# Two pairs of column blocks of the convolution's input computed with seven block products for eight at 9 of 32 channel pairs

## The reference

```python
h = rms_norm(x, norm_g[l])
proj = jnp.einsum('bsd,dn->bsn', h, w_in[l])
(aq, ak, av, ai, af, ao, az,
 bcq, bk, bv, bki, bwi, bz,
 cqkv, cb, ca, cz) = jnp.split(proj, split_points, axis=-1)
...
qkv = jax.nn.silu(causal_depthwise_conv(cqkv, d_conv_w[l]))
```

## Time and profile before

| | |
|---|---|
| median of 3 runs | 1528.72 us |
| the profiled execution's own time | 1529.63 us |
| its span | 1527.8 us |
| TensorE busy | 1523.5 us, 100%, 6960 matmuls |
| VectorE busy | 1044.1 us, 68% |
| ScalarE busy | 781.0 us, 51% |
| GpSimd busy | 362.9 us, 24% |
| read from HBM | 312.81 MB |
| granted TensorE clock, mean | 1.000 |

### The profile page before, as it was taken

One profiled execution on the slowest core, in us unless ns is written; L12 is line 12 of the kernel. 1 busy time (PEld: TensorE's weight loads), 2 busy tenths in 40 slices (PEclk: granted clock), 3 DMA queues, 4 the chain that ended last, 5 costly groups with the idle time before them and its releaser, 6 DMA issues.

```text
span 1527.8 us, 18922 instructions
## 1 busy us (share of the span) xinstructions
PE 1523.5 (100%) x6960; PEld 1261.3 (83%) x6960; DVE 1044.1 (68%) x1608; ACT 781.0 (51%) x1039; POOL 362.9 (24%) x608
## 2 busy tenths in 40 slices
PE   9999999999999999999999999999999999999999
PEld 7888888888888887888878888888888888888887
DVE  6647555666759865576569677676555877788883
ACT  6745444487544444554545545544445555454543
POOL 9041112230230030126420254344300011110000
PEclk9999999999999999999999999999999999999999
DMA  9886778886788875458765787798876677667667
GB/s 288 286 239 195 224 215 230 217 232 182 227 249 251 252 221 169 147 184 282 246 201 172 228 250 204 236 274 255 231 245 189 191 220 212 190 223 222 210 203 193
DMA packets 207980, 339.35 MB, mean 222 GB/s; under 512 B 53097, under 2 KB 60568, under 8 KB 207632
## 3 DMA queue, kind: packets, MB, share of 16 engines
q1 hardware_dynamic: 184784, 288.66, 62.1%
q0 software_dynamic: 23056, 49.47, 12.4%
q10 hardware_dynamic: 48, 0.02, 0.0%
HBM read 312.81 MB, written 28.73 MB: 224 GB/s over the span
## 4 chain that ended last, share of the span: by engine, by line
PE 98%; DVE 1%; ACT 0%; issue 0%; DMA 0%; DVEq 0%
PE acc L1186 29%; PE acc L1189 29%; PE acc L1188 28%; PE mix L1189 1%; PE mix L1188 1%; PE mix L1186 1%; PE mix L1293 1%; PE mix L1376 1%; PE acc L1202 1%; PE acc L1204 1%; PE acc L1203 1%; PE mix L1204 1%; PE mix L1203 1%; PE mix L1202 1%; PE mix L1365 0%; PE mix L1286 0%
## 5 line engine op out<-in xcount | busy, mean ns | idle before, releaser
L1879 DVE TENSOR_TENSOR w_lo<-w_raw,w_hi 128x1024 fp32r<-128x1024 f32 (+2 forms) x523 | 629.2, 1217 | 356.5 <-ACT w_hi L1517 352.9
L1517 ACT ACTIVATE w_hi<-w_raw 128x1024 fp32r<-128x1024 f32 (+2 forms) x523 | 542.9, 1049 | 436.9 <-PE acc L1189 346.1
L1186 PE MATMUL acc<-w_hi,op_hi 128*128 128x512 f32 (+1 forms) x1868 | 734.2, 393 | 0.3 <-DVE w_lo L1879 0.3
L1189 PE MATMUL acc<-w_hi,op_lo 128*128 128x512 f32 (+1 forms) x1868 | 726.9, 389 | 0.0
L1188 PE MATMUL acc<-w_lo,op_hi 128*128 128x512 f32 (+1 forms) x1868 | 726.7, 389 | 0.0
L1186 PEld LDWEIGHTS acc<-w_hi,op_hi 128*128 128x128 f32 x1868 | 350.8, 188 | 73.9 <-issue 1.3
L1189 PEld LDWEIGHTS acc<-w_hi,op_lo 128*128 128x128 f32 x1868 | 350.6, 188 | 73.5
L1188 PEld LDWEIGHTS acc<-w_lo,op_hi 128*128 128x128 f32 x1868 | 350.9, 188 | 70.8
L888 POOL DMA_DIRECT2D conv_dram<-y x48 | 30.6, 690 | 169.3 <-ACT y L1580 168.5
L888 POOL DMA_DIRECT2D y_dram<-y x32 | 20.6, 716 | 120.2 <-DVE y L2198 68.6
L1049 POOL DMA_DIRECT2D bp_dram<-b_ps x48 | 31.4, 712 | 67.4 <-ACT b_ps L1749 64.0
(11 more groups left out here) (455 smaller groups left out, 1312.4 us busy)
## 6 DMA issues: line engine op xcount, KB each, us to landing
w_raw<-in_w_in_dram SPq DMA_DIRECT2D x367, 512.0 KB, 4.6
w_raw<-in_w_out_dram SPq DMA_DIRECT2D x128, 512.0 KB, 4.5
w_raw<-in_w_in_dram SPq DMA_DIRECT2D x16, 384.0 KB, 3.3
w_raw<-in_a_wuq_dram SPq DMA_DIRECT2D x12, 512.0 KB, 5.7
out_dram<-in_x_dram POOLq DMA_DIRECT2D x7, 512.0 KB, 6.3
conv_dram<-y POOLq DMA_DIRECT2D x48, 64.0 KB, 3.9
y<-conv_dram POOLq DMA_DIRECT2D x48, 64.0 KB, 4.7
w_raw<-in_a_wuqi_dram SPq DMA_DIRECT2D x6, 512.0 KB, 4.7
```

The lines of the kernel that those rows point to most:

```text
L1186: nc.tensor.matmul(o, hi[:, kt, tok], hv[:, i, n0:n1], start=(kt == (kts if late else blk["kts"])[0]), stop=False)
L1189: last_mm = nc.tensor.matmul(o, lo[:, kt, tok], hv[:, i, n0:n1], start=False, stop=(kt == blk["kts"][-1]))
L1517: func(split_ap(w_hi, c), w_raw[:, c % RAW_BUFS, 0:n], ACT.Copy).then_inc(hi_ready, 1)
L1879: vec.tensor_tensor(split_ap(w_lo, c), w_raw[:, c % RAW_BUFS, 0:n], split_ap(w_hi, c).bitcast(F32), ALU.subtract).then_inc(lo_ready, 1)
```

## The change

conv 2 and 3, and conv 4 and 5, become two pairs as well. The first uses seven products at channel pairs 0 to 4, the second at 0 to 3, nine in all. `CONV_ORDER` gives the order of the chunks: 1 is a chunk of the pair's first column block alone, 2 one of the second, S a channel pair in both columns, with seven products. The first pair is chunks 32 to 63; its S pairs are chunks 36/37, 42/43, 48/49, 52/53, 56/57. The second is chunks 64 to 95, with S at 66/67, 72/73, 78/79, 84/85. The number of chunks and their bytes stay the same. For the sums of x VectorE first adds `op_hi` and `op_lo` again (`xs`), makes the four sums, ScalarE makes their high part (`xh`) and VectorE the low part (`xl`), for five channel pairs, in steps 17 to 27. The ScalarE pieces `evac` of conv 2 to 5 go; in their place come `evs` and `evx` (ScalarE scales the combined products, two operations of 128x1024) once per pair and `evn` on VectorE (two operations of 128x512) per column block. The gate for `cd` and `conv` moves with the end of the blocks.

```diff
-SEVEN = [[8, 9, 10, 11, 12], [8, 9, 10, 11, 12, 13, 14]]
+SEVEN = [[0, 1, 2, 3, 4], [0, 1, 2, 3], [8, 9, 10, 11, 12], [8, 9, 10, 11, 12, 13, 14]]
+CONV_SINGLE = 2
+CONV_ORDER = ["1211S1111S1112S22S22S122222", "12S1111S1111S1122S1222222222"]
+X_S = SEVEN[0]
...
-    for j in range(6):
+    for j in range(CONV_SINGLE):
         project("conv", j, C_CQKV + 512 * j)
+    for j in range(CONV_SINGLE, 6):
+        p, q = (j - CONV_SINGLE) // 2, (j - CONV_SINGLE) % 2
+        plain, seven = [i for i in range(KT // 2) if i not in SEVEN[p]], iter(SEVEN[p])
+        of_column = iter(plain)
+        kts = [2 * i + a for token in CONV_ORDER[p] if token in ("S", "12"[q])
+               for i in [next(seven) if token == "S" else next(of_column)] for a in range(2)]
+        block("cpair", j, "h", kts, wide, 512, "w_in", C_CQKV + 512 * j)
...
+        if x["kind"] == "cpair":
+            p, q = (x["arg"] - CONV_SINGLE) // 2, x["arg"] % 2
+            if q:
+                of_seven = [c for c, (b_, kts) in enumerate(chunks) if b_ == b and kts[0] // 2 in SEVEN[p]]
+                woven[of_seven[0] - 2].append(("four", p))
+                woven[of_seven[-1]] += [("evs", p), ("evx", p)]
+            woven[last[b]].append(("evn", (p, q)))
...
+    for n, i in enumerate(X_S):
+        for name, more in (("xs", 0), ("xh", 1), ("xl", 2)):
+            woven[NX + 1 + 2 * n + more].append((name, i))
+    at = 0
     for j in range(6):
-        at = weave((end("conv", j) if j else FIRST_EVAC) + (12 if j < 5 else 9), [("cd", 2 * j), ("cd", 2 * j + 1)])
-        at = weave(at, [("conv", 2 * j), ("conv", 2 * j + 1)], 3 if j < 5 else 2)
+        ended = (FIRST_EVAC, end("conv", 1))[j] if j < CONV_SINGLE else end("cpair", j)
+        at = weave(max(at, ended + (12 if j < 5 else 9)), [("cd", 2 * j), ("cd", 2 * j + 1)])
+        at = weave(at, [("conv", 2 * j), ("conv", 2 * j + 1)], 3 if j < 4 else 2)
...
+            def evx(p, use):
+                act.wait_ge(rstd_ready, 1)
+                if p == 0:
+                    for use in four_mix(p):
+                        act.wait_ge(emptied[use % 4], use // 4 + 1)
+                else:
+                    for q in range(2):
+                        wait_acc_read(act, p, q)
+                for m in range(M):
+                    func(pair_sum(p)[:, m], pair_sum(p)[:, m], ACT.Copy, scale=rstd[:, m:m + 1]).then_inc(pair_scaled, 1)
...
+            def xs_sums(i, use):
+                raw = x_raw(i)
+                hi, lo = [v[:, 2 * i:2 * i + 2, :].rearrange("p k t -> p (k t)") for v in (op_hi, op_lo)]
+                step(vec.tensor_tensor(raw, hi.bitcast(F32), lo.bitcast(F32), ALU.add))
+                a11, a21, a12, a22 = [raw[:, P * j:P * j + P] for j in range(4)]
+                step(vec.tensor_tensor(a22, a21, a22, ALU.add))
+                step(vec.tensor_tensor(a21, a11, a21, ALU.subtract))
+                step(vec.tensor_tensor(a11, a22, a11, ALU.subtract))
+                vec.tensor_tensor(a12, a12, a11, ALU.subtract).then_inc(s_summed, 1)
...
+                if p < 2:
+                    dve.wait_ge(pair_scaled, M * (p + 1))
+                    dve.wait_ge(conv_summed, 2 * (2 * p + q + 1))
...
+                    if p < 2:
+                        ins = vec.scalar_tensor_tensor(conv_stage(CONV_SINGLE + 2 * p + q)[:, m], plain_banks(p)[k],
+                                                       rstd[:, m:m + 1], dst, ALU.mult, ALU.add)
```

More of the change, by code:

```diff
@@ L159, in plan @@
     for b, blk in enumerate(blocks):
-        second = blk["kind"] == "pair" and blk["arg"] % 2
+        second = blk["kind"] in ("pair", "cpair") and blk["arg"] % 2
+        if blk["kind"] == "cpair":
+            if second:
+                p, place = (blk["arg"] - CONV_SINGLE) // 2, [0, 0]
+                for token in CONV_ORDER[p]:
+                    for q in range(2):
+                        if token in ("S", "12"[q]):
+                            b_ = b - 1 + q
+                            chunks.append((b_, blocks[b_]["kts"][2 * place[q]:2 * place[q] + 2]))
+                            place[q] += 1
+                for b_ in (b - 1, b):
+                    last.append(max(c for c, (own, _) in enumerate(chunks) if own == b_))
+            continue
         if second:
@@ L558, in pair_of, with in_pair @@
         def pair_of(c):
-            return blocks[chunks[c][0]]["arg"] // 2 - OUT_SINGLE // 2
+            blk = blocks[chunks[c][0]]
+            return (blk["arg"] - CONV_SINGLE) // 2 if blk["kind"] == "cpair" else 2 + (blk["arg"] - OUT_SINGLE) // 2
+        def in_pair(c):
+            return blocks[chunks[c][0]]["kind"] in ("pair", "cpair")
         def in_seven(c):
-            b, kts = chunks[c]
-            return blocks[b]["kind"] == "pair" and kts[0] // 2 in SEVEN[pair_of(c)]
+            return in_pair(c) and chunks[c][1][0] // 2 in SEVEN[pair_of(c)]
         def second_col(c):
@@ L584, in seven_banks @@
         def seven_banks(p):
-            return [bank(use)[:] for use in four_mix(0)] if p == 0 else four_acc()
+            return [bank(use)[:] for use in four_mix(p)] if p % 2 == 0 else four_acc(p)
         def pair_block(p):
-            return next(b for b, x_ in enumerate(blocks) if x_["kind"] == "pair" and x_["arg"] == OUT_SINGLE + 2 * p)
-        def s_hi(i):
+            kind, arg = ("cpair", CONV_SINGLE + 2 * p) if p < 2 else ("pair", OUT_SINGLE + 2 * (p - 2))
+            return next(b for b, x_ in enumerate(blocks) if x_["kind"] == kind and x_["arg"] == arg)
@@ L675, in wait_filled @@
         def wait_filled(eng, use):
-            eng.wait_ge(filled[use % 4], use // 4 + 1)
+            unsignalled = sum(use > use_of["four", p] for p in range(2))
+            eng.wait_ge(filled[use % 4], use // 4 + 1 - unsignalled)
         def wait_emptied(eng, use):
@@ L690, in wait_stored @@
         def wait_stored(eng, kind, arg=0):
+            if kind == "conv" and arg >= CONV_SINGLE:
+                p, q = (arg - CONV_SINGLE) // 2, arg % 2
+                if p == 0:
+                    wait_acc_read(eng, p, q)
+                else:
+                    for use in four_mix(p)[2 * q:2 * q + 2]:
+                        eng.wait_ge(emptied[use % 4], use // 4 + 1)
+                return
             b = next(i for i, x_ in enumerate(blocks) if x_["kind"] == kind and x_["arg"] == arg)
```

143 lines of the change are left out of this document (93 added, 50 removed).

## The result

| | before | changed |
|---|---|---|
| median | 1528.89 us (1528.32 to 1529.62, 4 runs) | 1550.45 us (1548.63 to 1552.83, 4 runs) |
| the profiled execution's own time | 1529.63 us | 1549.96 us |
| its span | 1527.8 us | 1548.2 us |
| matmuls | 6960 | 6933 |
| granted TensorE clock, mean | 1.000 | 0.994 |

The change makes the kernel slower by 1.42%: ratio 1.0142, 95% interval 1.0124 to 1.0159. The forecast was 1545.6 us with 1538 to 1552 around it. The sign and the range held; the median lies 4.9 us above the forecast.

A forecast was written before the change was run, and what follows sets the result against it. TensorE's list was taken to bound the kernel (98% of the chain of waits). Waits of 22.96 us less 6.12 us of matmuls made 16.8 us longer, 1545.6 us against 1528.72, with a range of 1538 to 1552.

The forecast's parts named there:

- The gain: TensorE's list: nine channel pairs with 21 matmuls for 24, 27 x 0.2267 = 6.12 us less.
- The mechanism: VectorE's queue: convolution pieces ahead of an S pair's chain cost their length less a 0.64 us margin; before, 5.47 us hid them.
- The waits: TensorE waiting at S pairs and some plain chunks of the convolution's column blocks: 22.96 us in sum.
- The clock: TensorE's clock at the new gaps: nothing in the sum, three chunks at the lower level, 8 us, in the bounds.
- the likeliest case: The whole kernel: the forecast's own case, 1542 to 1549 us from landing times and signal delays, chance 0.66.
- rival 3: TensorE's clock falls at the gaps of 48/49, 52/53 and 78/79: 1548 to 1554 us; chance 0.12.
- The sums of x at nothing: VectorE, steps 17 to 27: 2.6 us for each of five pairs costs nothing; up to 2.3 us without the cushion.
- The weights' DMAs in the landing time alone: Weight loads: same number and bytes, priced only through the 4.7 us landing time; 3.8 gives waits of 21.2, 5.5 gives 25.4.
- Rival 1: Convolution pieces hide in VectorE's 32% idle time, the S pairs' chain fits, only the gain is left: 1522.6 us; chance 0.08.
- Rival 2: TensorE's waits: delays overlap more, the five largest shrink by 45%, waits 15 us, time 1537.6 us; chance 0.12.
- Rival 4: Whole kernel: nothing moves, gain and waits cancel as TensorE's waits fall to 6 us: 1528.7 us; chance 0.02.
- After 300 us both run level: Traces of both kernels after 300 us: should run level, with no size given.

The follow-up runs named there:

- short waits: Against the kernel before, without S pairs in the convolution: five of the twelve turns of the head work made nine times instead of once; 1545.22 us, ratio 1.0105.

## Why the prediction was right, and what was off

- **The gain**, 27 x 0.2267 = 6.12 us: right. With it taken at this size, the accounts of the two kernels that bear on it most, two S pairs fewer and the order that hides nearly all waits, close within 0.4 us.
- **The mechanism**, pieces in VectorE's queue ahead of an S pair's chain with a margin of 0.64 us: right, and shown from both sides. Taking the taps away took 19 us off; moving one by a step moved the waits nearly as laid out; moving all, with the chunks, took 25.8 us off with no work removed.
- **The waits**, forecast 22.96 us, measured 18.7. Place by place, forecast and measured: 42/43 1.96 and 1.81; 45 0.96 and 0.78; 48/49 4.73 and 4.32; 52/53 3.55 and 1.02; 66/67 0.83 and none over 0.45; 72/73 none and 0.73; 78/79 4.62 and 2.12 + 2.60; 84/85 2.30 and 1.66; 87 0.96 and 0.76; 89 2.83 and 2.88; 56/57 and 61 0.10 and 0.12, none over 0.45. One place makes most of the difference, 52/53: the slow matmuls from 149.18 on delay TensorE by some 2.4 us, and VectorE catches up meanwhile, as the part on the clock said it might. With fewer slow matmuls at 48/49 more stayed of it: 1.74 us with 8 of them (two S pairs fewer), 1.78 with 7 (sums of x left out), 1.02 with 11.
- **The clock** is the step that was mis-sized. The forecast said "I put nothing in the sum and three such chunks, 8 us, in the bounds". Measured: 32 matmuls at the lower level, 6.4 us, and with the restarts 8.0 us of late starts, so the 8 us in the bounds had the right size and the nothing in the sum had not. By the text's own test ("or if the granted clock is below 1.00 there") the likeliest case was wrong in this: what came is rival 3, the same mechanism with falls of the clock, at 48/49 and 78/79 as it named them, but at 89 and not at 52/53. 1550.45 us lies in its 1548 to 1554 and not in the 1542 to 1549 of the case with 0.66. 8.0 us of late starts left out and 4.3 us of waits too many make 3.7 us; the profiled execution's 1549.96 exceeds the 1546.4 by 3.6. The rest of the 4.9 us is chance between executions: it lies in the step from one execution to the median, taken as 0.8 us down, where the changed kernel's median lies 0.5 us above its profiled execution.
- **The sums of x at nothing**: right, with a run of its own.
- **The weights' DMAs in the landing time alone**: right in kind, but one landing time for all of them was too simple. No wait of TensorE is put down to them, yet ScalarE waits for `w_raw` in eight places between 98 and 280 us, 14.8 us in all, where before it never did, and VectorE in two, 0.54 and 0.39 us. At 48/49 the landing in the chain took 4.41 us where 4.7 was assumed. At 72/73, where no wait was foreseen, it took 7.14 us (202.43 to 209.57), and the chain of the 0.73 us there leads back to it. VectorE and ScalarE at that place:

```profile
209.66 1.23 DVE L1988 TENSOR_TENSOR y<-w_raw 128x1024 f32<-128x1024 f32 x1 [0.39 <-DMA w_raw<-in_w_in_dram]
```

```profile
209.59 0.63 ACT L1593 ACTIVATE w_hi<-w_raw 128x512 fp32r<-128x512 f32 x1 [1.57 <-DMA w_raw<-in_w_in_dram]
```

- **Rivals 1, 2 and 4** fall with the changed profile. Rival 1's argument, that the average of the stretch is near balance, was sound in itself: with another order the time is 1524.7 us, 2 from its 1522.6. It was the order of the work, not its amount.
- **After 300 us both run level**: right, the lag is 20.39 us at 293 us and 20.4 at the end.

The Trainium skill ("TensorE: Matmul & The Clock Gate", Part 1) says that an idle array goes back to half clock until it has been busy again. The traces agree that it falls behind waits, and to that level (0.43 us a start for 0.23). They also show waits of 2 to 2.9 us without a fall. The same part of the Trainium skill says that the chip's observation of the engine runs freely, not from the program's start; that would let equal waits end differently, but no run here shows it.

## What to carry to other kernels

A step that hides more than one chunk deep can lose its cover when the operation behind it gets a longer chain: work out the margin of the new chain (here 0.64 us for 5.47) and look for everything that stands ahead of it in the queue, on both engines. Averages of busy time said that it fits, and with another order it did; so before such a change is given up, lay the queues out and move the pieces and the chunks together, since moving one piece only moved the wait. And a wait of TensorE costs more than its length: with restart and clock these cost 1.1 to 1.4 times their sum.

## What the runs showed of the hardware

- After a wait the first matmul's successor starts 0.31 to 0.34 us later for 0.23, even where the clock stays up (178.41 to 178.74 above gives 0.33).
- A fall lasts 6 to 14 matmuls of 128x512 at 0.43 us (0.41 where the gates' matmuls have 496 columns), 1.2 to 2.8 us of loss, whatever the wait's length: 8 behind one of 1.97 us, 6 behind one of 4.37, and the longest, 14, behind the pair of 2.1 and 2.6 us in the run with one piece a step later.
- Falls by wait, in the profiled executions: none behind any single wait of up to 1.8 us; 2 of 5 at 1.9 to 2.0 us; of four of 2.8 to 2.9 us those in the changed kernel and in the run without the sums of x, and not those with one piece a step later (the same chunk) and with the pieces moved; behind the three double waits of 1.8 to 2.1 and 2.6 us at 78/79 each time, and always at 3.8 us and more, 10 of 10. So a wait of 2 to 3 us can't be priced better than with and without a fall. These counts are of one execution of each kernel, and others of the same kernel differ: the mean granted clock of the change's four is 0.994 to 0.997, that of the short waits' four 0.995 to 0.998, and with the taps left out one execution in ten has 0.999, though none of its waits is over 1.82 us in the profiled one.
- A slow TensorE gives time to an engine that is late: the wait at 52/53 is 1.02 us behind 11 slow matmuls and 1.74 and 1.78 behind 8 and 7, so falls and waits must be added along the timeline and not by themselves.
